# A mixture-of-experts tail in one kernel: one scatter per pair of items, the last 2 MB of weights by output column, and a pair loop that begins with the odd item

## The reference

```python
hb = xpad[tok] @ mlp1_w[e] + mlp1_b[e]            # 1024 -> 2048
yb = clamped_swiglu(hb) @ mlp2_w[e] + mlp2_b[e]   # 1024 -> 1024
return yb * wr[:, None].astype(yb.dtype)          # wr: the token's gate
...
y = jax.ops.segment_sum(ys.reshape(R, D), row_tok, num_segments=T + 1)[:T]
```

## Time and profile before

| what | us |
| --- | --- |
| median of 3 runs (1249.6 to 1250.23) | 1250.0 |
| the profiled execution, its own time | 1248.68 |
| its span, first to last instruction | 1246.8 |

### The profile page before, as it was taken

How to read it: one execution, slowest core, us unless ns; L and a number is a source line. 1 busy time by engine, 2 the same in 40 slices (tenths; PEclk the granted TensorE clock), 3 DMA queues, 4 the chain that set the end, 5 groups by cost and what they waited for, 6 DMA issues and landing times.

```text
span 1246.8 us, 19008 instructions
## 1 busy us (share of the span) xinstructions
PE 1211.5 (97%) x7700; PEld 612.0 (49%) x7700; DVE 373.3 (30%) x855; ACT 191.1 (15%) x435; POOL 76.8 (6%) x118
## 2 busy tenths in 40 slices
PE   9999999999999999999899999999999898989998
PEld 8888778888844343324334343443333232333332
DVE  4457784314064121212122122221212121212111
ACT  2332357214110000000000000000000000000001
POOL 7210012010100000000000001000000000000000
PEclk9999999999999999999999999999999999999999
DMA  7333212394789999999999999999999999999997
GB/s 267 135 137 132 103 37 71 141 427 175 304 340 425 427 428 429 437 429 432 430 433 432 433 430 432 429 432 431 435 423 430 432 433 433 429 429 429 429 427 308
DMA packets 27982, 442.46 MB, mean 355 GB/s; under 512 B 3104, under 2 KB 3232, under 8 KB 5664
## 3 DMA queue, kind: packets, MB, share of 16 engines
q1 hardware_dynamic: 27072, 440.23, 83.9%
q10 hardware_dynamic: 864, 1.57, 0.4%
HBM read 440.75 MB, written 1.05 MB: 354 GB/s over the span
## 4 chain that ended last, share of the span: by engine, by line
PE 75%; DMA 21%; DVE 2%; ACT 1%; issue 1%; SPq 0%; ACTq 0%; POOL 0%; DVEq 0%; POOLq 0%
PE ps L1010 29%; DMA sb_ring<-in_mlp_w 21%; PE ps L1052 11%; PE ps L332 8%; PE ps L986 3%; PE ps L976 3%; PE ps L832 2%; PE ps L783 2%; PE ps L692 2%; PE ps L998 2%; PE ps L1038 1%; PE ps L345 1%; PE ps L567 1%; PE ps L433 1%; PE ps L416 1%
## 5 line engine op out<-in xcount | busy, mean ns | idle before, releaser
L1010 PE MATMUL ps<-sb_ring,sb_xv 128*64 128x512 f32 x2048 | 455.7, 597 | 23.7 <-DMA sb_ring<-in_mlp_w 23.5
L1010 PEld LDWEIGHTS ps<-sb_ring,sb_xv 128*64 128x64 f32 x2048 | 142.1, 137 | 312.0 <-issue 279.6
L1052 PE MATMUL ps<-sb_ring,sb_xv 128*64 128x512 f32 x1024 | 227.0, 595 | 0.3
L1656 DVE TENSOR_SCALAR sb_early<-ps 128x256 f32<-128x256 f32 x64 | 27.2, 425 | 625.1 <-PE ps L1010 619.8
L1052 PEld LDWEIGHTS ps<-sb_ring,sb_xv 128*64 128x64 f32 x1024 | 72.7, 137 | 131.1 <-issue 129.0
L1697 ACT ACTIVATE sb_early<-sb_early 128x256 f32<-128x256 f32 (+2 forms) x69 | 28.2, 408 | 507.1 <-DVE sb_early L1656 500.7
L1697 ACT ACTIVATE sb_early<-ps 128x512 f32<-128x512 f32 (+2 forms) x39 | 21.1, 543 | 274.8 <-PE ps L1052 265.0
L986 PE MATMUL ps<-sb_early 64*128 64x512 f32 x248 | 61.6, 615 | 0.0
L332 PE MATMUL ps<-sb_hnT,sb_wsl 128*128 128x256 f32 x256 | 56.1, 379 | 0.0
L976 PE MATMUL ps<-sb_early,sb_hnT 128*128 128x128 f32 x480 | 56.0, 275 | 0.0
L976 PEld LDWEIGHTS ps<-sb_early,sb_hnT 128*128 128x128 f32 x480 | 54.8, 192 | 0.0
(11 more groups left out here) (370 smaller groups left out, 1015.5 us busy)
## 6 DMA issues: line engine op xcount, KB each, us to landing
sb_ring<-in_mlp_w SPq DMA_DIRECT2D x55, 4096.0 KB, 19.1
sb_ring<-in_mlp_w SPq DMA_DIRECT2D x54, 2048.0 KB, 17.5
sb_ring<-in_mlp_w SPq DMA_DIRECT2D x11, 3072.0 KB, 15.6
sb_wsl<-in_w_front SPq DMA_DIRECT2D x31, 1024.0 KB, 4.8
sb_ring<-in_mlp_w SPq DMA_DIRECT2D x10, 1024.0 KB, 7.5
sb_wsl<-in_mlp_w SPq DMA_DIRECT2D x3, 1024.0 KB, 8.9
sb_spare<-in_mlp_w SPq DMA_DIRECT2D x2, 1024.0 KB, 9.3
sb_ring<-in_mlp_w SPq DMA_DIRECT2D x4, 512.0 KB, 13.0
```

The source lines that it names most:

```text
L1010: mm = pe.matmul(psum[64 * half:64 * half + 64, 4 + n, :], xgT[:, k, SLOTS * par:SLOTS * par + SLOTS], ring[:, at + 512 * half:at + 512 * ...
L1052: mm = pe.matmul(psum[64 * o2:64 * o2 + 64, 7, :], actT[:, 2 * n + m, 64 * q:64 * q + 64], ring[:, at + 512 * o2:at + 512 * o2 + 512], sta ...
L1656: dve.tensor_scalar(gl, psum[:, 4 + n, 0:256], 7.0, None, ALU.min).then_inc(sem("glu"), 1)
```

## The change

1. **Scatter.** An item's result is copied from bank 7 to two `yb` buffers by halves of the partitions, so that `yb[0]` and `yb[1]` hold the left and the right output columns of both items of a pair. The gates' transposes go to `selgT` in the same way. `scatter` is called once per pair, in the even item after `hidden(n=0)`, with four matmuls that contract over 128 partitions. The halves of the odd items' results lie exchanged in bank 7 (`rows(par, o2)`). ACT's copy of 128 partitions becomes two of 64, DVE's copy of the gates too.
2. **Order in an item.** `turn_act(0)` goes into the middle of `hidden(n=1)`. `second_open` works on p4, with `turn_act(1)` in its middle, and comes ahead of `gather`; p5 follows the gather.
3. **Layout of p5.** Its 2 MB lie in HBM and in `ring` by output column: the left 256 columns of both halves of the output first, then the right 256. In all items but the last, a matmul on p5 reads 2 x 256 columns that lie 2048 numbers apart.
4. **The last item.** `second_open` writes its left and right 256 columns to banks 7 and 4 (sixteen matmuls of 256 columns in place of eight of 512); the left side closes after the first half of p5, the right side after the second; each side is scattered as soon as it is closed and copied, the left one between the two last quarters. The right side's scatter waits until DVE and ACT have taken the left side of banks 0 to 3. Eight stores of 128 KB take the place of four of 256 KB.
5. **The stream.** PE adds `h` into banks 1 and 3 alone, now between items 30 and 31. DVE adds `h` to banks 0 and 2 when it takes them.
6. **Loops.** PE runs item 0, then a loop over (odd item, even item of the next pair), then item 31. The item table's last steps (`item_table`) go on DVE from item 0's end to its middle. `yb[1]`, `gate4` and `gateT` lie in `smalls`.

```diff
-            def scatter(par):
+            def scatter(cols=slice(0, 512)):
...
                     for o2 in range(2):
-                        r = slice(64 * o2, 64 * o2 + 64)
-                        mm = pe.matmul(psum[:, 2 * tt + o2, :], selgT[par][r, tt, :], yb[r, :],
+                        mm = pe.matmul(psum[:, 2 * tt + o2, cols], selgT[o2][:, tt, :], yb[o2][:, cols],
                                        start=False, stop=False, skip_group_check=True)
-                mm.then_inc(sem("scattered"), 1)
+                    if cols.stop - cols.start < 512:
+                        mm.then_inc(sem("scattered"), 1)
...
+                        if k == 3 and n:
+                            if first:
+                                pe.wait_ge(sem("gate_taken"), 1)
+                            turn_act(i, 0)
+                        elif k == 3 and last and par:
+                            turn_gates(i)
...
+            def rows(par, o2):
+                return slice(64 * (par ^ o2), 64 * (par ^ o2) + 64)
+
+            def second_open(i, par, first=False, late=False):
+
+                pe.wait_ge(sem("act_out"), i * 2 + 2)
+                landed(i, 4, first)
+                for q in range(2):
+                    if q:
+                        turn_act(i, 1)
+                        if late:
+                            pe.wait_ge(sem("late_in_0"), 16)
                     for m in range(2):
+                        at = 16384 + 2048 * q + 1024 * m
+                        for bank, cols in ((7, slice(0, 256)), (4, slice(256, 512))) if late else ((7, slice(0, 512)),):
+                            for o2 in range(2):
+                                mm = pe.matmul(psum[rows(par, o2), bank, cols],
...
+            def second_close(i, par, side, qs, bank=7):
+
+                for q in qs:
+                    for m in range(2):
+                        at = 20480 + 2048 * side + 1024 * q + 512 * m
+                        for o2 in range(2):
+                            mm = pe.matmul(psum[rows(par, o2), bank, 256 * side:256 * side + 256],
...
+            def last_scatter(side):
+
+                pe.wait_ge(sem("y_out"), last_pair * 2 + 3 + side)
+                pe.wait_ge(sem("y_low"), side + 1)
+                if side:
+                    pe.wait_ge(sem("out_left"), 2)
+                    pe.wait_ge(sem("out_right"), 2)
+                scatter(slice(256 * side, 256 * side + 256))
...
                 hidden(i, par, 0, first, last)
+                if not par and not first:
+                    pe.wait_ge(sem("y_out"), i + 1)
+                    scatter()
...
                 if last and par:
...
+                    second_open(i, par, late=True)
+                    pe.wait_ge(sem("act_out"), i * 2 + 3)
+                    landed(i, 5, first)
+                    second_close(i, par, 0, (0, 1)).then_inc(sem("half_used"), 1)
+                    pe.wait_ge(sem("late_in_1"), 16)
+                    second_close(i, par, 1, (0,), bank=4)
+                    last_scatter(0)
+                    pe.wait_ge(sem("late_in_2"), 16)
+                    second_close(i, par, 1, (1,), bank=4).then_inc(sem("piece_used"), 1)
+                    last_scatter(1)
                     return
-                turn_act(i, 0)
...
-                else:
-                    scatter(1 - par)
-                turn_act(i, 1)
+                second_open(i, par, first)
                 if par:
                     pe.wait_ge(sem("selected"), j + 3)
                     gather()
-                for n in range(2):
-                    second(i, n, (0, 1), first)
...
             item(0, 0, first=True)
-            item(0, 1)
...
-            with pe.Fori(1, last_pair) as j:
-                for par in range(2):
-                    item(j, par)
-            for bank in range(4):
+            with pe.Fori(0, last_pair) as j:
+                item(j, 1)
+                item(j + 1, 0)
+            for bank in (1, 3):
...
-            for par in range(2):
-                item(last_pair, par, last=True)
...
+            item(last_pair, 1, last=True)
```

DVE's side of the last item (ACT does the same with banks 1 and 3 in `right_half`, with a plain copy, and issues the store of each itself):

```diff
+            for side in range(2):
+                cols = slice(256 * side, 256 * side + 256)
...
+                dve.tensor_copy(yb[1][0:64, cols], psum[0:64, 4 if side else 7, cols]).then_inc(sem("y_low"), 1)
+                for tt in range(TT):
+                    dve.wait_ge(sem("scattered"), 2 * side + tt + 1)
+                    dve.tensor_tensor(h[:, tt, cols], psum[:, 2 * tt, cols], h[:, tt, cols], ALU.add) \
+                       .then_inc(sem("out_left"), 1)
```

More of the change, by code:

```diff
@@ L206, in build @@
         selg, sel = view(early, 768, TT, P), view(early, 1024, TT, PAIR)
-        selgT = [view(early, 1280 + 256 * par, TT, P) for par in range(2)]
-        gate4, gateT = view(early, 1536, TT, 4, NE), view(early, 1536, TT, P)
-        yb = view(early, 1792, 512)
+        selgT = [view(early, 1280 + 256 * o2, TT, P) for o2 in range(2)]
+        gate4, gateT = view(smalls, 0, TT, 4, NE), view(smalls, 0, TT, P)
+        yb = [view(early, 1792, 512), view(smalls, 0, 512)]
         bias1, bias2 = view(early, 2304, 512), view(early, 1792, 512)
@@ L1666, in item @@
                         dve.wait_ge(sem("gated_turned"), i + 2)
-                        dve.tensor_copy(selgT[par], view(psum[:, 7, 0:256], 0, TT, P)).then_inc(sem("selgT"), 1)
+                        low, high = slice(0, 64), slice(64, 128)
+                        dve.tensor_copy(selgT[par][low], view(psum[low, 7, 0:256], 0, TT, P))
+                        dve.tensor_copy(selgT[1 - par][high], view(psum[high, 7, 0:256], 0, TT, P)).then_inc(sem("selgT"), 1)
+                        if first:
+                            item_table()
                 light(i + 1)
@@ L1995, in _, with item @@
             f(gateT, view(psum[:, 6, 0:256], 0, TT, P), ACT.Copy).then_inc(sem("gate_taken"), 1)
-            def item(i, last=False):
+            def item(i, par, last=False):
                 def gate_half(n):
@@ L2019, in _ @@
-            item(0)
-            act.wait_ge(sem("tabled"), 1)
-            last_item = act.value_load(tabi[0:1, 62:63], min_val=NE - 1, max_val=ITEMS)
-            with act.Fori(1, last_item) as i:
-                item(i)
-            item(last_item, last=True)
+                    act.wait_ge(sem("half_used"), 4)
+                    f(yb[0][64:128, 0:256], psum[64:128, 7, 0:256], ACT.Copy).then_inc(sem("y_out"), 1)
+                    for tt in range(TT):
+                        right_half(0, tt)
@@ new lines, in item, with right_half @@
+                act.wait_ge(sem("piece_used"), i * PIECES + PIECES)
+                if last:
+                    f(yb[0][64:128, 256:512], psum[64:128, 4, 256:512], ACT.Copy).then_inc(sem("y_out"), 1)
+                else:
+                    f(yb[par][0:64, :], psum[0:64, 7, :], ACT.Copy)
+                    f(yb[1 - par][64:128, :], psum[64:128, 7, :], ACT.Copy).then_inc(sem("y_out"), 1)
+            def right_half(side, tt):
+                lo = 256 * side
+                cols = slice(512 + lo, 512 + lo + 256)
+                act.wait_ge(sem("scattered"), 2 * side + tt + 1)
+                f(h[:, tt, cols], psum[:, 2 * tt + 1, lo:lo + 256], ACT.Copy).then_inc(sem("out_right"), 1)
+                act.wait_ge(sem("out_right"), 2 * side + tt + 1)
+                act.dma_start(out[0, tt * P:(tt + 1) * P, cols], h[:, tt, cols]).then_inc(sem("out_done"), 16)
@@ L2025, in _ @@
+            item(0, 0)
+            item(1, 1)
+            act.wait_ge(sem("tabled"), 1)
+            last_pair = act.value_load(tabi[0:1, 0:1], min_val=NE // 2 - 1, max_val=(ITEMS + 1) // 2 - 1)
+            with act.Fori(1, last_pair) as j:
+                for par in range(2):
+                    item(j * 2 + par, par)
+            item(last_pair * 2, 0)
+            item(last_pair * 2 + 1, 1, last=True)
             for tt in range(TT):
-                act.wait_ge(sem("scattered"), last_item + 2 + 2 * tt)
@@ L2278, in _ @@
             piece(e, PIECES - 1, at=(24576 - 1024, 24576), name="late_in_2")
-            for tt in range(TT):
-                sp.wait_ge(sem("out_left"), tt + 1)
-                sp.dma_start(out[0, tt * P:(tt + 1) * P, 0:512], h[:, tt, 0:512]).then_inc(sem("out_done"), 16)
-            sp.wait_ge(sem("out_done"), 64)
+            for side in range(2):
+                cols = slice(256 * side, 256 * side + 256)
+                for tt in range(TT):
+                    sp.wait_ge(sem("out_left"), 2 * side + tt + 1)
+                    sp.dma_start(out[0, tt * P:(tt + 1) * P, cols], h[:, tt, cols]).then_inc(sem("out_done"), 16)
+            sp.wait_ge(sem("out_done"), 128)
 _INS = ["x_T", "mem_T", "smalls", "lora", "w_front", "w_values", "mlp_w", "mlp_b1", "mlp_b2"]
```

90 lines of the change are left out of this document (33 added, 57 removed).

## The result

The changed kernel takes 1256.3 us (median of 6 runs, 1252.89 to 1258.65) against 1250.12 us (6 runs, 1249.6 to 1251.19): a ratio of 1.005, interval 1.004 to 1.006. It is slower, by 6.2 us, and outside the range of the prediction. Its runs lie further apart than those of before. The profiled execution took 1258.65 us, with a span of 1256.6: 9.8 us more than the 1246.8 of before.

What follows compares the result with a forecast made beforehand. The weight stream was taken to bound the kernel until p3 of item 31, PE's tail after it. Loop changes 0, tail +0.7 us (span 1247.5 against 1246.8), with the median 1.3 above the profiled run: 1250.7 us, range 1248.2 to 1252.8.

Steps and rivals of the forecast that it cites:

- All of it lies beneath the stream: worth 0: Pair's scatter in the loop: saves 0.21 us of PE per pair, 3.2 us over 15 pairs, hidden by weight loads.
- PE has 2.2 us per item to spare where the stream is full: 0: Order in an item: a full item takes 29.1 us to load, PE at most 26.9, so reordering costs 0.
- What it gains there it waits away before 1110: 616 to 909 us: any lead PE builds over the stream there is lost in waits for weights before 1110 us.
- PE's time per pair: Expert loop: scatter 3.63 us per pair in place of 3.84, stalls of 0.1 us per item at most.
- The change of shape: Left scatter in the last item: 0.15 us added for changing tiling mode between matmuls 64 wide.
- The stall for `turn_act(1)`: Inside `second_open`: 8 records, 1.8 us, ahead of it against 1.84 for the SwiGLU; 0.1 us per item at most.
- p4's wait for landing comes 3.6 us sooner in odd items: Odd items in the loop: PE needs p4 earlier; priced at 0 with the order in an item.
- PE's pace counts after all: Rival, chance 0.05: scatters save 3.2 us and additions 1.8, less stalls; 1248.9 us with the tail.
- The dear records of 256 columns: Rival, chance 0.10: 64 records behind p3 at 0.185 us each cost 4.2 us more, 1254.9 us.
- the clock falling in the tail: Rival, chance 0.05: after PE's wait for p3 the clock drops, costing 1.7 us, 1252.4 us.
- The tail: From p3 of item 31: PE is the bound, last store issued at 1244.88, span ends 1247.54 against 1246.8, +0.7 us.
- PE's gain of 0.35 at p3: Two fewer additions of `h` let PE begin p3 of item 31 at 1228.55 in place of 1228.90.

Runs made afterwards that it cites:

- The doses: Kernel before with gates' transposes and odd items' first-half activation transposes done twice, then three times: 1252.7 us, then 1255.1 us.
- The kernels without early loads: Kernel before and changed kernel, both without the 1 MB early loads and GpSimd's copies, items 6 to 27 in 4 MB loads: 1276.0 and 1275.5 us.
- the merged order: Changed kernel with full 128 x 128 matmuls brought together, four changes of shape per pair where it had seven: 1251.37 us.
- the last version: Changed kernel with even items in merged order, odd items' gather halved around `turn_act(1)` before all of second, last pair scattered singly: 1248.05 us.
- the single scatters: Changed kernel with items 30 and 31 each scattered alone, over 64 partitions: 1257.75 us; p3's start to span's end 17.6 us in place of 18.9.
- the first dose: Kernel before with gates' transposes done twice in each item and those of the activations' first half twice in odd items: 1252.7 us.
- the two comparisons that bear on the waits alone: Changed kernel with items 10 to 20's p2 to p5 in 2 MB loads: 1254.08 us; merged order plus single scatters, 1250.81, against the last version, 1248.05.

## Why the prediction was wrong

**The step that failed** is the price of PE's time in the stage from 616 to 909 us: "All of it lies beneath the stream: worth 0", and for the order "PE has 2.2 us per item to spare where the stream is full: 0". The text had two numbers, 26.9 us of PE for an item and 26.8 of stream, and read them as a stream that sets the pace whatever PE does. The 26.9 was worked out from the stream's own 430 GB/s, so it could not have come out otherwise; PE's chain, 53.76 us for a pair, gives the same 26.9 by itself. It is a balance. The ring holds one item, so a stream ahead of PE has to stop, and it does: DMA share 0.12. "What it gains there it waits away before 1110" is true for a gain. A loss isn't made good later, because from 909 us on the stream runs at its full rate (431 GB/s to 1110 us, where it had 432 before) and has no rate left to catch up with. So the last landing came 7.9 us later, where the prediction took more than 2 us as a sign that it was wrong. The doses put a price on it: 3.1 and 5.4 us for 0.66 and 1.31 us more per pair. The kernels without early loads show the other side, where the changed order cost nothing that could be seen.

**PE's time per pair** was forecast at 0.21 less plus at most 0.2 of stalls, and came 0.74 more. The scatter's 3.63 was right. The change of shape was seen: the sum has it, with 0.15 us, for the tail. It was left out of the loop, where the change adds three of them per pair; and merging three gave 0.95 us, thus 0.3 each. The stall for `turn_act(1)` was up to 0.2 per item, where the sum had at most 0.1. The Trainium skill's rule ("TensorEngine Tiling (Array Packing)", Key Properties: a change of tiling mode drains the engine) bears on it, and the merged order agrees with it in sign; the size is the runs', not the page's.

**The landings of p4.** "p4's wait for landing comes 3.6 us sooner in odd items" was written down and priced at 0. In the changed kernel p4 and p5 of an odd item are needed 16.0 us after their place was freed (from 712.34 + 3.43, where `piece_used` is counted for p5, to 731.73, where `hidden(1)` ends, in the chain above; the 15.4 written down ahead of the last version was wrong), and PE waited for them in 4 places of the stage. The version with the halved gather, which spreads the two kinds of item to 19.2 and 19.7, has no such wait.

**The rivals.** "PE's pace counts after all" named the right mechanism and had a chance of 0.05. It was priced with PE getting faster, so it stood on the side of the gains. The dear records of 256 columns didn't come: with weights 64 wide they cost 1.88 / 16 = 0.117 us a record, where the sum had 0.12.

**The clock.** The prediction had a rival with the clock falling in the tail; the tail kept the full clock. It did fall in three places ahead of it, each time behind a wait of 2.2 us: to 0.83, 0.79 and 0.79 over the 8 to 10 us at 1010, 1070 and 1128 us, where 8 records of `second_open` took 2.3 to 2.9 us in place of 1.9. After the first two PE still found waits further on. The third follows PE's last wait for weights; for comparison, a wait in the stage of the loss with the clock at 1.00 behind it:

```profile
786.97 1.94 PE L1056 MATMUL ps<-sb_ring,sb_xv 128*64 128x512 f32 x8 [0.76 <-DMA sb_ring<-in_mlp_w]
...
1128.85 2.94 PE L1056 MATMUL ps<-sb_ring,sb_xv 128*64 128x512 f32 x8 [2.20 <-DMA sb_ring<-in_mlp_w]
```

From that start to the gather it is 5.70 us (1128.85 to 1134.55) where it is 4.10 at the other (786.97 to 791.07). PE finds no wait behind it in which these 1.6 us could be made up, and is 1.3 us late for p3. So the 0.9 us by which it was later there than in the kernel before are, by this estimate, the clock's in this one execution.

**The tail** went as summed: 19.0 us from p3 to the end, measured 18.9, each step within 0.3 us. The left scatter began at 1248.1, behind the last landing (`late_in_2`, 1246.4), so nothing hid it, and the pair's second item cost 1.3 us there, as the single scatters show. PE's gain of 0.35 at p3 didn't come: PE was 1.3 us late for it, since it ran from 1128 us on without a wait, at 27.25 us for an item, and the clock fell at the start of that.

**Open.** The runs of the changed kernel lie 6 us apart, and the profiled one is the longest of them. That holes differ from run to run fits, but only one execution of each kernel has a trace. The clock may have a part in it: the fastest run, 1252.89, is the only one of the six with a mean granted clock of 1.000, and so is the fastest of the kernel with single scatters in its tail (1252.59); the others, at 0.992 to 0.998, show no order. No run tells whether the full clock made them fast or the lack of waits kept it full. How the 6.2 us divide is an estimate and not measured: some 3.1 for PE's pace (the first dose makes a pair about as long as the change does, 54.42 for 54.50), 0.95 for the tail, which leaves some 2 for the waits; the two comparisons that bear on the waits alone give 1.7 and 2.7.

## What to carry to other kernels

When two streams of work run at the same pace, neither has slack: price an edit by the stage's own two rates (here 26.9 against 26.8 us for an item), and ask how far the one may run ahead of the other before a buffer of fixed size stops it. A loss in a balanced stage stays to the end if the stages behind it run at the limit of the other engine. On PE, count how often the shape of the matmuls changes along the loop, and put transposes, scatters and gathers side by side; and see to it that a buffer's slots are asked for again at even distances.

## What the runs showed of the hardware

A change from matmuls with weights 64 wide to full 128 x 128 ones and back cost about 0.3 us each when three were taken out of a pair (54.50 to 53.55). Four matmuls over 128 partitions (8 records, 3.63 us) and eight over 64 (16 records, 3.84), do the same scatter in nearly the same time, so the pairing gained almost nothing by itself. A stage can show a DMA share of 0.99 and still have moved 2.3% fewer bytes than one at 1.00 (420 GB/s for 430), so the GB/s tell more than the share does. Behind three waits of 2.2 us of PE the granted clock was 0.79 to 0.83 for some 8 us; behind the waits of 0.64 to 1.23 us, and one of 2.2 us at 622 us, it was not seen to fall.
